# Two layers and a retrieval layer on one core: first input loaded transposed, first weight chunk in quarters, rows in groups of two, one branch product moved, head 0 decoded in two halves

## What is computed

```python
def hybrid_layer(x, ...):                       # twice
    proj = x @ w_in                             # queries, keys, values, gates, recurrent columns
    y = concatenate([retention * silu, nsa * silu, rg_lru * silu]) @ w_out
    return layer_norm(ALPHA * x + y)
# then: x1 = x + gate * ((sigmoid(gm) * (m @ w_m) + sigmoid(ga) * (a @ w_a)) @ w_out)
#   m: mLSTM output, a: attention output ("branches")
# then, with h = modulated rms norm of x1, for each of 8 heads:
#   s1, s2 = scores of h's query against 128 + 128 sub keys
#   top 16 of each; sums of the 16 x 16 pairs; top 16 of these: expert = 128 * i1 + i2
#   weight = softmax(sum) * gelu(h . u[expert])
#   out = x1 + gate * sum over heads and choices of weight * v[expert]
```

## Time and profile before

| | |
|---|---|
| median of three runs | 1359.69 us (1356.15 to 1364.97) |
| the profiled execution's own time | 1359.75 us |
| its span, first to last instruction | 1358.2 us |
| mean granted TensorE clock | 0.959 |
| first gather issued | 690.39 us |
| last gathered row read by VectorE | 1346.74 us |

### The profile page before, as it was taken

How to read it: one execution, slowest core, us unless ns; L and a number is a source line. 1 busy time by engine, 2 the same in 40 slices (tenths; PEclk the granted TensorE clock), 3 DMA queues, 4 the chain that set the end, 5 groups by cost and what they waited for, 6 DMA issues and landing times.

```text
span 1358.2 us, 14573 instructions
## 1 busy us (share of the span) xinstructions
PE 1196.2 (88%) x5168; PEld 722.9 (53%) x5168; DVE 855.1 (63%) x2197; ACT 298.5 (22%) x941; POOL 311.9 (23%) x278
## 2 busy tenths in 40 slices
PE   7999799989999989998899889889777878778777
PEld 4976558857855757764466444445333333233233
DVE  2645954365542658685287677777777777767655
ACT  1114300243210233231123222222211121111111
POOL 0000000000000010000044354454554444445430
PEclk9999999999999998998999899999998888899998
DMA  8561145731343453544369999999999999999994
GB/s 358 222 249 62 63 180 192 282 125 63 124 170 141 154 194 125 196 145 186 124 246 421 422 421 422 421 421 422 421 421 421 422 422 421 422 421 421 422 421 180
DMA packets 49143, 385.83 MB, mean 284 GB/s; under 512 B 5680, under 2 KB 7472, under 8 KB 9392
## 3 DMA queue, kind: packets, MB, share of 16 engines
q0 software_dynamic: 36864, 268.45, 47.6%
q1 hardware_dynamic: 12208, 116.46, 22.9%
HBM read 383.85 MB, written 1.05 MB: 283 GB/s over the span
## 4 chain that ended last, share of the span: by engine, by line
PE 57%; DMA 31%; DVE 7%; ACT 3%; issue 2%; POOL 0%; SPq 0%; DVEq 0%; ACTq 0%
PE bank L518 23%; DMA arena<-peer_uv_in,arena 14%; PE bank L524 14%; PE bank L1111 11%; DMA wring<-peer_uv_in,arena 10%; DMA const<-peer_uv_in,arena 5%; PE bank L559 2%; DVE arena L1565 1%; PE bank L749 1%; DVE arena L2218 1%; DVE arena L1573 1%; PE bank L591 1%; PE bank L662 1%; ACT hT L1211 1%; PE bank L915 1%
## 5 line engine op out<-in xcount | busy, mean ns | idle before, releaser
L1111 PE MATMUL bank<-arena 128*128 128x512 f32 x460 | 223.7, 626 | 40.8 <-ACT arena L1533 40.7
L518 PE MATMUL bank<-wring,hT 128*128 128x256 f32 (+2 forms) x656 | 195.0, 455 | 6.8 <-ACT hT L1211 4.2
L1111 PE MATMUL bank<-wring,arena 128*128 128x512 f32 x340 | 166.4, 628 | 39.0 <-ACT arena L1533 39.0
L524 PE MATMUL bank<-hT,wring 128*128 128x256 f32 (+1 forms) x1088 | 189.8, 334 | 0.5 <-ACT hT L1211 0.4
L524 PEld LDWEIGHTS bank<-hT,wring 128*128 128x128 f32 x1088 | 170.3, 193 | 25.8 <-issue 10.5
L2218 DVE CUSTOM_DVE_ANT_0 arena<-arena 128x1024 f32<-128x1024 f32 x115 | 140.9, 1226 | 67.4 <-DMA arena<-peer_uv_in,arena 67.3
L1111 PEld LDWEIGHTS bank<-arena 128*128 128x128 f32 x460 | 88.6, 200 | 160.4 <-issue 102.0
L2304 POOL DMA_INDIRECT arena<-peer_uv_in,arena x115 | 128.5, 1118 | 166.6 <-PE bank L1111 130.2
L2282 POOL TENSOR_TENSOR small<-small,const 128x1 f32<-128x1 f32 (+3 forms) x18 | 16.1, 896 | 651.5 <-DVEq L1577 293.5
L518 PEld LDWEIGHTS bank<-wring,hT 128*128 128x128 f32 x656 | 123.3, 191 | 70.6 <-issue 53.3
L2218 DVE CUSTOM_DVE_ANT_0 wring<-wring,arena 128x1024 f32<-128x1024 f32 x85 | 104.1, 1225 | 53.3 <-DMA wring<-peer_uv_in,arena 53.2
(11 more groups left out here) (208 smaller groups left out, 1263.7 us busy)
## 6 DMA issues: line engine op xcount, KB each, us to landing
wring<-w_in SPq DMA_DIRECT2D x22, 2048.0 KB, 8.1
wring<-ada_in SPq DMA_DIRECT2D x12, 2048.0 KB, 8.8
wring<-wo_in SPq DMA_DIRECT2D x5, 2048.0 KB, 8.2
wring<-cmp_in SPq DMA_DIRECT2D x2, 2048.0 KB, 8.9
wring<-br_in SPq DMA_DIRECT2D x2, 2048.0 KB, 8.4
arena<-pq_in SPq DMA_DIRECT2D x2, 2048.0 KB, 10.2
wring<-pq_in SPq DMA_DIRECT2D x2, 2048.0 KB, 8.7
wring<-w1b_in SPq DMA_DIRECT2D x2, 1120.0 KB, 8.6
```

The costliest lines, as they stand in the source:

```text
L518: ins = pe.matmul(bank[:, 0:cols], lhs[k], w[:, k, 0:cols], start=(k == 0), stop=(k == n - 1))
L524: ins = pe.matmul(bank[:, at:at + n_tok], w[:, k, col:col + P], rhs[:, k, :], start=(k == 0), stop=(k == KC - 1))
L1111: ins = pe.matmul(sums_of[half][:, :], diag[:, at % NDIAG, :], v_row[slot_of[at]][:, half * 512:(half + 1) * 512], start=(n == 0), stop=(n ...
```

## The change

It does five things.

1. The host hands over `xT` as an array of its own. SyncE loads it in two halves of K, each ahead of two quarters of the first weight chunk, and `first_query_rows` multiplies both token tiles slice by slice of K as they come. The transposes and copies of layer 0 go. The identity comes with the other constants. `x` itself, first read near the end of layer 0, is loaded once, ahead of `cond`. `arrival` counts the ring's semaphores, since the first chunk no longer raises that of its slot.
2. Three of the attention branch's products stay in the loop; the fourth (half 1, tile 1) stands behind it, ahead of `latent_transposes(0)`. VectorE's readers take the same order.
3. Head 0: part 7 finds positions before it removes values; `decode(0, "idx_first")` decodes the first eight right after part 7, then come parts 8 and 9 and `decode(8, "idx_ready")`. GpSimd's first gather waits for `idx_first` alone, its ninth for `idx_ready`.
4. All groups have two rows, but the last two of one: 127 groups of 2.
5. `GROUP` is 2, the width of the small buffers.

```diff
-        sizes = [2] * 48 + [4] * ((ROWS - 100) // 4) + [2, 1, 1]
+        sizes = [2] * (ROWS // 2 - 1) + [1, 1]
...
+        def arrival(chunk):
+
+            s, nth = place[chunk]
+            return nth + (0 if s == place[("w1", 0, 1)][0] else 1)
...
+                def first_query_rows():
+
+                    w = slot(("w1", 0, 1)).rearrange("p (k c) -> p k c", k=KC)
+                    two = [job(("rqk", 0, t)) for t in range(TT)]
+                    for k in range(KC):
+                        if k % 4 == 0:
+                            pe.wait_ge(sem(f"in_xT{k // 4}"), 16)
+                        if k % 2 == 0:
+                            pe.wait_ge(sem(f"w_first{k // 2}"), 16)
+                        for t in range(TT):
+                            ins = pe.matmul(two[t][:, :], xT[:, k, t * P:(t + 1) * P], w[:, k, :], start=(k == 0), stop=(k == KC - 1))
+                            if k == KC - 1:
+                                finish(ins, ("rqk", 0, t))
...
-                    branch("ba", aT, (n - 4) // 2, n % 2)
+                    branch("ba", aT, n % 2 if n < 6 else 0, n // 6)
...
-                    between(i + 1)
+                    if i < 6:
+                        between(i + 1)
...
+            branch("ba", aT, 1, 1)
             latent_transposes(0)
...
-                half, t = divmod(n, 2)
+                t, half = divmod(n, 2)
...
-            for part in range(16):
+            for part in range(8):
                 choose(0, part)
+            decode(0, "idx_first")
+            for part in (8, 9):
+                choose(0, part)
+            decode(TOPK // 2, "idx_ready")
...
+            def decode(lo, done):
+
+                n = TOPK // 2
+                k = slice(lo, lo + n)
+                pair_of = lambda buf: buf.rearrange("p (a k) -> p a k", a=2)[:, :, k]
+                hots = [b[:, lo * TOPK:(lo + n) * TOPK].rearrange("p (k a) -> p k a", k=n) for b in (hot, hot_b)]
...
+                for j in range(2):
+                    step(tt(hots[j], hots[j], every(topf[:, j * TOPK:(j + 1) * TOPK], n), ALU.mult))
...
+                stt(idx[:, k], sel1[:, k], float(NKEY), sel2[:, k], ALU.mult, ALU.add).then_inc(sem(done), 1)
```

More of the change, by code:

```diff
@@ L49 @@
 SLOTS = 18
-GROUP = 4
+GROUP = 2
 NDIAG = 8
@@ L505, in weights @@
             def weights(chunk):
-                s, nth = place[chunk]
-                pe.wait_ge(w_full[s], 16 * (nth + 1))
+                s = place[chunk][0]
+                pe.wait_ge(w_full[s], 16 * arrival(chunk))
                 return slot(chunk)
@@ L1247, in _ @@
             for L in range(DEPTH):
-                for t, half in ((0, 0), (0, 1), (1, 0)):
+                for t, half in ((0, 0), (0, 1), (1, 0)) if L else ():
                     bank = full(act, ("xT", L, t, half))
@@ L1861, in first_rows @@
                 def first_rows(q):
+                    if L == 0 and q == 0:
+                        dve.wait_ge(sem("in_x"), 16)
                     bank = full(dve, ("wq", L, q))
@@ L2196, in choose @@
                     stt(idx[:, s * TOPK:(s + 1) * TOPK], sel1, float(NKEY), sel2, ALU.mult, ALU.add).then_inc(sem("idx_ready"), 1)
+            def decode(lo, done):
[3 more added lines that the diff above has]
+                hots = [b[:, lo * TOPK:(lo + n) * TOPK].rearrange("p (k a) -> p k a", k=n) for b in (hot, hot_b)]
+                iota = const[:, C_IOTA:C_IOTA + TOPK]
+                settle()
+                step(ts(bhl[:, k], bpos[:, k], 4, ALU.logical_shift_right))
+                step(ts(bhl[:, TOPK + lo:TOPK + lo + n], bpos[:, k], TOPK - 1, ALU.bitwise_and))
+                settle()
+                step(dve.tensor_copy(pair_of(fhl), pair_of(bhl)))
+                settle()
+                for j in range(2):
+                    step(tt(hots[j], every(fhl[:, j * TOPK + lo:j * TOPK + lo + n], TOPK, 2), every(iota, n), ALU.is_equal))
+                settle()
+                for j in range(2):
+                    step(tt(hots[j], hots[j], every(topf[:, j * TOPK:(j + 1) * TOPK], n), ALU.mult))
+                settle()
+                for j, sel in enumerate((sel1, sel2)):
+                    step(dve.tensor_reduce(sel[:, k], hots[j], AX.X, ALU.add))
+                settle()
+                stt(idx[:, k], sel1[:, k], float(NKEY), sel2[:, k], ALU.mult, ALU.add).then_inc(sem(done), 1)
             def choice_weights(head):
```

66 lines of the change are left out of this document (30 added, 36 removed).

## The result

The changed kernel took 1342.59 us (median of 4 runs, 1336.45 to 1345.44), the kernel before 1359.07 (4 runs). The medians differ by 16.5 us where 11.2 were predicted, and the time lies outside the range. Built and run again it was 0.989 (0.9866 to 0.9915). The profiled execution, 1336.45 us (span 1334.6), is the fastest of its four, 6 us under their median; before's was at its median.

What follows compares the result with a forecast made beforehand. The prediction took DMA to bound the gathers from 700 to 1338 us, and TensorE or its hand-overs the stages before. Its terms, -3.4 - 4.7 - 1.9 - 2.0 + 0.8 = -11.2 us, gave 1348.5 from 1359.75; range 1344 to 1354.

Steps and rivals of the forecast that it cites:

- Start, -3.4: First input: transposed x and quartered weights save 3.4 us, by dropped transposes and an earlier first product; bounds -2.0 to -5.6.
- the 1.4 us for what lay ahead of the product: Kernel start: 576 KB less to load ahead of the first product, at 422 GB/s, starts it 1.4 us sooner.
- the 2.0 for the transposes: Kernel start: without transposes, copies and waits between them, the two first products take 16.6 us instead of 18.59, saving 2.0.
- the bound of -5.6: Kernel start, far bound: the first two pieces land fast enough to start the products near 5.7 us instead of 7.95.
- Branch product, -4.7: Behind the mLSTM loop: the moved product fills TensorE's wait (1.6 us) and keeps its clock up (3.1); bounds -1.6 and -4.7.
- The 3.1 us for the clock: Two products behind the mLSTM loop take 7.0 us at full clock instead of 10.12, since TensorE's long pause goes.
- Head 0, -1.9: Before the gathers: decoding the first eight positions early brings the first gather 1.9 us sooner; bounds 0 and -2.5.
- the fifth gather: Issued after TensorE's last product; the four gathers ahead were to keep DMA busy until its first byte, just covering it.
- tail -2.0: Kernel end: with groups of two, TensorE's last row starts 2.0 us sooner; bounds 0 and -2.3.
- Cost 0: Gathering stretch: 39 added groups at about 1.1 us each hide in VectorE's waits for rows, so cost nothing.
- The +0.8 for the lagging engine: End of the gathers: more instructions, guessed to load through the one late DMA engine, add 0.8 us; bounds 0 and +2.
- more than the sum: Rival, chance 0.14: the start reaches its -5.6 bound or the lagging engine gets no later; 1345.5 us.

Runs made afterwards that it cites:

- before_later: The kernel before with TensorE's first transposes made to wait for 12 small VectorE operations on a free buffer; ratio to before 1.0021.
- slots_up_160: The kernel before with 40 unused floats ahead of three gather slots, moving them up 160 bytes to a multiple of 256; ratio to before 0.9981.
- whole_without_start: The changed kernel with the old start: x loaded in rows and transposed on TensorE, weights in halves; ratio to before 0.9932.
- whole_later: The changed kernel with TensorE's first product made to wait for 15 small VectorE operations on a free buffer; ratio to before 0.9929.
- its two halves: The kernel before with groups of two but GROUP left at 4 (0.9995), and with only three slots moved to multiples of 256 by padding (0.9981).
- only_mid: The kernel before with only the branch product moved behind the mLSTM loop; ratio to before 0.9970.
- only_head: The kernel before with only head 0's decode split in two; ratio to before 0.9975.

## Why the prediction was wrong

**Start, -3.4: under.** The columns start at 26.8 us in the mean of nine profiles with the old start (24.9 to 27.8, before_later left out) and at 22.4 in eight with the new one (21.7 to 23.1; the two that begin late on purpose left out): -4.5. The step that failed is the 1.4 us for what lay ahead of the product: the first product starts at 8.8 us in the mean of the nine and at 6.4 in that of the eight, 2.4 sooner (3.1 between before and after themselves), while the 2.0 for the transposes was right (18.0 us from there to the columns, 15.9 after). The 1.4 took the old start as pieces that follow one another at full rate; but by the trace's landings half of the sixteen engines had their share of the first half chunk at 6.75 us and the last at 9.21. In the nine old starts the last engine lands it anywhere from 6.9 to 9.6 us, in six of them after 8.9; the new start's first quarter is complete at 6.1 to 6.8 in all. In the changed kernel's own profile the bound of -5.6, which had the first product at 5.7 us, was nearer (6.25).

**Branch product, -4.7: right mechanism, 4.1.** The wait is gone, and the pair takes 7.13 us in all ten profiles with the part and 8.5 to 10.1 in the ten without. The 3.1 us for the clock were those of before's own profile; over the others it is 1.4 to 3.0.

**Head 0, -1.9: right**, 1.8, and the fifth gather is covered.

**Groups: tail -2.0 right** (4.83 to 2.9). **"Cost 0" in the gathering stretch: wrong**, and this is the step that matters: I costed the added instructions, which were covered, and did not ask what else GROUP sets. It moved three slots by 96 bytes, worth 2.3 to 3.7 us of the stretch. The +0.8 for the lagging engine can't be read in the sum, since the alignment hides it: at equal places the stretch is longer with groups of two, 656.8 and 657.1 against a mean of 656.4 (655.9 to 657.0) with the slots of before, a mean of 653.9 against 652.9 with those of after, and 647.46 against 647.00 with all aligned. That is 0.5 to 1 us in these few profiles, of the size of their scatter. One engine still works nearly alone at the end (share 0.06 from 1318 to 1325); the prediction guessed that it loads instructions besides, and the packets of q14 went from 30 to 33, but no run tests this.

The sum with measured terms is -4.5 - 4.1 - 1.8 - 2.6 - 2.0 = -15.0 us, where -2.6 is the whole change of the stretch, in place of the prediction's 0 + 0.8. Measured are -16.5 (-13.3 to -22.3 by the interval of the ratio). Of the 3.8 us by which the sum was short the stretch makes 3.4 and the start 1.1; branch product and head 0 were 0.7 too high.

**What is left lies between 28 and 620 us.** From the columns to the pair after takes 600.2 us, before 608.8, of which the product explains 2.4. The difference grows in jumps, where the granted clock falls. This one, 64 products of one stage, is of before (windows 400:440 and 440:460 at 0.93 and 0.97):

```profile
438.19 15.58 PE L524 MATMUL bank<-hT,wring 128*128 128x256 f32 x64
```

and this of slots_up_160, whose program is before's with 40 floats of padding (1.00 and 1.00):

```profile
436.43 14.06 PE L525 MATMUL bank<-hT,wring 128*128 128x256 f32 x64
```

The same 64 products take 15.58, 16.73 (before_later) or 14.06 us (slots_up_160, whole_without_start, after) by where the clock falls. Both starts show both kinds: 604.9 to 611.6 us from columns to pair with the old one, 600.2 to 608.7 with the new. The new start lies lower by more than the product. In this stretch TensorE is at the lower clock for 30.7 to 48.5 us in the ten profiles with the old start (mean 38.3, summed from the traces' clock records) and for 23.9 to 37.5 in the ten with the new one (mean 29.0), and on the whole the stretch is the longer the more of it there is. What decides number and place of the falls was not found, and delaying the new start did not bring them back (27.3 us in whole_later). It stays open, as does a second point: alone the groups part measured -7.9 us, while its two halves measured -0.7 and -2.6; it also moves the diagonals' buffer, which no run moved alone.

Of the prediction's rivals "more than the sum" was the one that came. Of its two causes the start went half the way to its far bound in the mean of the profiles, and the engine not later isn't shown; the larger cause, the alignment, it did not name. That its time of 1345.5 lies near the measured one is in part luck.

## What to carry to other kernels

A constant that sizes a buffer also places all that is allocated behind it: list the addresses before and after, and where a stretch is bound by transfers into SBUF, begin every destination at a multiple of 256 bytes (here 9.35 us of 656 for one argument of the allocator and 96 bytes of padding). Read a step of 2 to 4 us in the stretch that it changes and across several profiles; totals whose single runs differ by 10 us don't show it. Before taking a load's landing as its cost, look whether fifteen engines had it long before the sixteenth.

## What was not expected of the hardware

- A packet of 8192 bytes into SBUF takes 309 ns at a multiple of 256 bytes and mostly 311 to 322 beside one; 128 above a multiple is no better than 96. With all at a multiple the sixteen engines gather at 426 to 427 GB/s, with none at 421 to 422.
- The first half chunk lands on fifteen engines by 7.05 us and on the sixteenth at 9.21 in before, on all by 6.92 in whole_without_start; nothing in the program differs there. In other executions more are late: three in only_mid (9.13 to 9.22), ten in before_later (7.42 to 9.02).
- A program moved by 5.5 us at its start is 5.9 us later at its first gather: the falls of the granted clock move with the program (the five falls ahead of the first gather each begin some 6.1 us later). Yet two executions of nearly the same program lose it at different places, 3 to 5 us apart by 630 us.
- From the first gather to the last row TensorE spends 64.8 to 99.0 us at the lower clock with groups of four and 20.5 to 34.1 with groups of two, which give it shorter pieces and shorter pauses (3.70 and 1.2 us in the groups at the end above; in before around 1250 us mostly 7.1 to 7.3 and 2.3 to 3.8). While DMA bounds, that brings nothing; but with groups of four the last row came 6.5 to 6.6 us behind in three profiles (in only_head the clock falls there, and eight of the last records take 5.32 us where the next eight take 3.60), with groups of two never more than 3.0.
